# Prompt attention by residue, with inputs split beforehand and outputs scaled from PSUM by VectorE

## Reference

```
q_f, k_f, v_f, logf, dil, gate_a, gate_b = project(x)   # 8 heads of 64; 3 dilated groups (window, r)
# forget-gated prompt attention: c = cumsum(logf)
s = q @ k.T * 64**-0.5 + c[q] - c[k];  o_fox = softmax(s, k <= q) @ v
# dilated prompt attention, groups (128, 1), (512, 4), (2048, 16):
# a query sees keys of its own residue mod r, at most window behind, then groups are merged
o_g, lse_g = band_attn(...);  o_dil = sum_g softmax_g(lse_g) * o_g
h = x + (sigmoid(gate_a) * (o_fox @ Wa) + sigmoid(gate_b) * (o_dil @ Wb)) @ W_out
y = h + relu(rmsnorm(h) @ W_up)**2 @ W_down
```

## Time and profile before

| | us |
|---|---|
| median of 3 runs (range) | 1779.7 (1779.42 to 1780.15) |
| span of the profiled execution | 1779.2 |
| what lies around the span | about 0.5 |
| last sample product to first prompt product | 1068.28 to 1072.42 |
| first product of `finish` | 1255.98 |

### The profile page before, as it was taken

How to read it: one execution, slowest core, us unless ns; L and a number is a source line. 1 busy time by engine, 2 the same in 40 slices (tenths; PEclk the granted TensorE clock), 3 DMA queues, 4 the chain that set the end, 5 groups by cost and what they waited for, 6 DMA issues and landing times. The chain is left out here.

```text
span 1779.2 us, 32332 instructions
## 1 busy us (share of the span) xinstructions
PE 1710.8 (96%) x10749; PEld 1529.3 (86%) x10749; DVE 1086.7 (61%) x2480; ACT 956.5 (54%) x1649; POOL 868.4 (49%) x496
## 2 busy tenths in 40 slices
PE   6999999999889999999999977898999999999998
PEld 5888888899889999899899956888998989899897
DVE  6747556422388888888888877888444514234251
ACT  5444344432368887888888877988314313122230
POOL 1615233300338878778788747775233433333332
PEclk9999999999999999999999998999999999999999
DMA  7386585645889999999999976320645566666662
GB/s 238 106 290 216 202 300 183 207 132 137 253 308 365 344 351 350 353 347 336 355 360 349 316 232 163 91 73 25 215 146 214 235 259 236 259 236 260 236 259 77
DMA packets 191563, 427.76 MB, mean 240 GB/s; under 512 B 22761, under 2 KB 86122, under 8 KB 190002
## 3 DMA queue, kind: packets, MB, share of 16 engines
q1 hardware_dynamic: 187474, 415.29, 66.8%
q10 hardware_dynamic: 2560, 8.39, 1.6%
q0 software_dynamic: 1376, 2.10, 0.5%
HBM read 392.36 MB, written 120.64 MB: 288 GB/s over the span
## 5 line engine op out<-in xcount | busy, mean ns | idle before, releaser
L1086 POOL TENSOR_TENSOR vv_lo<-v_raw,vv_hi 128x1024 fp32r<-128x1024 f32 x178 | 401.4, 2261 | 147.9 <-ACT vv_hi L1175 145.7
L1986 POOL TENSOR_TENSOR w_lo<-w_raw,w_hi 128x2048 fp32r<-128x2048 f32 x39 | 180.1, 4619 | 318.4 <-ACT w_hi L2000 318.4
L1167 ACT ACTIVATE kt_hi<-ktp 128x1024 fp32r<-128x1024 f32 (+1 forms) x192 | 186.2, 970 | 94.0 <-PE ktp L1351 93.2
L1191 DVE TENSOR_TENSOR kt_lo<-ktp,kt_hi 128x1024 fp32r<-128x1024 f32 (+1 forms) x192 | 220.9, 1151 | 8.1 <-ACT kt_hi L1167 6.2
L1365 PE MATMUL s_ps<-kt_hi,q_st 128*128 128x256 f32 (+3 forms) x768 | 205.9, 302 | 0.8 <-DVE mx_parts L1241 0.4
L1351 PE MATMUL ktp<-ident,k_raw 128*128 128x128 f32 x1440 | 192.0, 276 | 8.3 <-DVEq L1182 3.8
L1351 PEld LDWEIGHTS ktp<-ident,k_raw 128*128 128x128 f32 x1440 | 168.6, 142 | 32.7 <-issue 5.6
L707 PE MATMUL acc<-w_hi,xn_hi 128*128 128x512 f32 x480 | 192.4, 401 | 2.4 <-POOL w_lo L340 2.4
L1175 ACT ACTIVATE vv_hi<-v_raw 128x1024 fp32r<-128x1024 f32 (+1 forms) x192 | 191.4, 997 | 6.2 <-PE o_ps L1381 5.7
L1365 PE MATMUL s_ps<-kt_lo,q_st 128*128 128x256 f32 (+3 forms) x768 | 191.0, 282 | 0.0
L707 PE MATMUL acc<-w_lo,xn_hi 128*128 128x512 f32 x480 | 187.7, 391 | 0.0
(11 more groups left out here) (244 smaller groups left out, 4139.4 us busy)
## 6 DMA issues: line engine op xcount, KB each, us to landing
k_raw<-in_cache_fox_k SPq DMA_DIRECT2D x256, 256.0 KB, 4.9
v_raw<-in_cache_fox_v SPq DMA_DIRECT2D x256, 256.0 KB, 4.6
out_win_kv_sample<-in_cache_win_kv SPq DMA_DIRECT2D x32, 2040.0 KB, 9.5
w_raw<-in_w_in SPq DMA_DIRECT2D x32, 1024.0 KB, 5.9
k_raw<-in_cache_win_kv SPq DMA_DIRECT2D x40, 512.0 KB, 9.5
v_raw<-in_cache_win_kv SPq DMA_DIRECT2D x40, 512.0 KB, 8.6
w_raw<-in_w_up SPq DMA_DIRECT2D x16, 1024.0 KB, 5.3
w_raw<-in_w_down SPq DMA_DIRECT2D x16, 1024.0 KB, 5.1
```

Source lines behind the costliest of these rows:

```text
L1086: gp.tensor_tensor(vv_lo[:, slot, 0:tiles, :], v_raw[:, i % RAW_RING, 0:tiles, :], vv_hi[:, slot, 0:tiles, :].bitcast(F32), ALU.subtract). ...
L1167: act.activation(kt_hi[:, slot, :, 0:n], ktp[:, i % 2, :, 0:n], ACT.Copy).then_inc(k_hi, 1)
L1191: ve.tensor_tensor(kt_lo[:, slot, :, 0:n], ktp[:, i % 2, :, 0:n], kt_hi[:, slot, :, 0:n].bitcast(F32), ALU.subtract).then_inc(k_lo, 1)
L1986: gp.tensor_tensor(w_lo[slot][:], w_raw[:, slot, :], w_hi[slot][:].bitcast(F32), ALU.subtract).then_inc(slab_lo_done, 1)
```

## The change

**Residues.** In `project_tokens`, sets 2 and 3 are written with the prompt tokens of one residue mod 4 next to each other (`token_cols`, `turned_cols`). In `attend_prompt` those sets then score only a tile of 128 queries of one residue against the 128 keys of the same residue: 4 tiles a set and head in place of 10. Set 3 (r = 16) keeps a mask inside the tile. A head has 8 + 7 + 10 = 25 tiles, in 7 steps of up to 512 columns (`GROUPS`): two "spread" (sets 2 and 3), two "near" (set 1), three "far" (the forget-gated branch).

**Split inputs.** `project_tokens` stores the transposed queries and keys, and the values, as hi and lo parts. ACT writes y_hi in place of `y_t`; DVE gets a new subtraction of 128x512 out of PSUM a tile for y_lo; for values ACT gets one more copy and DVE one more subtraction a tile. `attend_prompt` splits no input; POOL's queue loads the parts, double-buffered for keys and values. The first pair, with 2 x 1 MB of zeros for the unused halves of the queries, is issued by POOL in `attend_sample` (`first_pair`).

**Outputs.** Probabilities aren't scaled any more. Near and spread have different row orders, so their maxima and sums are merged through DRAM: `send_near`, `take_near`, small operations on DVE, POOL and ACT, `send_shares`, `take_shares`, which brings the reciprocals to all partitions. DVE scales the near and far outputs as it takes them out of PSUM; ACT copies the spread output and POOL scales and adds it, once a pair.

```diff
+SPREAD, NEAR, FAR = 0, 1, 2
+GROUPS = ((SPREAD, (0, 1)), (SPREAD, (2, 3)), (NEAR, (2, 3)), (NEAR, (0, 1)), (FAR, (3,)), (FAR, (2,)), (FAR, (0, 1)))
+S_BANKS, T_BANKS = 3, 2
+SPREAD_BEHIND, NEAR_BEHIND, FAR_BEHIND = (6, 7, 9), (10, 11), (12, 13)
+KEEP_BEHIND, EXP_P_BEHIND, TURN_BEHIND, LOW_BEHIND = 1, 2, 4, 5
 # project_tokens, DVE
+            def turned_rows_lo(s, c, t, by_residue):
+                ve.wait_ge(yt_done, at + 3)
+                ve.tensor_tensor(token_cols(y_lo, t, by_residue), turned_cols(tp[:, slot, :], by_residue),
+                                 token_cols(y_hi, t, by_residue).bitcast(F32), ALU.subtract).then_inc(ylo_done, 1)
...
+                        if c and t < Q_TILES:
+                            turned_rows_lo(s, c - 1, t, by_residue)
+                        if c == 2 and t < Q_TILES:
+                            ve.wait_ge(vhi_done, 4 * s + t + 1)
+                            ve.tensor_tensor(v_lo[:, t, :], acc[:, t, :], v_hi[:, t, :].bitcast(F32), ALU.subtract).then_inc(vlo_done, 1)
 # project_tokens, PE, turn(s, c, t)
+                if at >= 2:
+                    pe.wait_ge(ylo_done, lows_done(at - 2))
 # attend_sample, POOL
+            def first_pair(b, i):
+                if b < DEC_BATCH - 1 or i < LAST:
+                    return
+                done(gp, s_done, group_index(b, LAST))
+                hold(gp)
+                load_keys_of(gp, a, ahead, 0)
+                load_queries(gp, a, ahead, 0, 0)
+                gp.dma_start(ahead["q"][64:128, :, 0].rearrange("p c s n -> p c (s n)"), a["c_zero"].bitcast(F32R)).then_inc(ahead["zeroed"], 16)
+                load_queries(gp, a, ahead, 0, 1)
+                gp.dma_start(ahead["q"][0:64, :, 1].rearrange("p c s n -> p c (s n)"), a["c_zero"].bitcast(F32R)).then_inc(ahead["zeroed"], 16)
 # attend_prompt, SP
+            def send_near(h, i):
+                if i == 0:
+                    sp.wait_ge(exp_done, STEPS * h + 4)
+                    sp.dma_start(a["stat_s"][h].rearrange("c (q p) -> p (c q)", p=P), ...)
...
+            straight(HEADS, STEPS, (6, send_near), (7, take_near), (8, bias_ahead),
+                     (10, send_far), (12, send_shares), (13, take_shares))
 # attend_prompt, POOL
+            def load_values(p):
+                for x, part in ((v_hi, "vh_s"), (v_lo, "vl_s")):
+                    for s in range(SETS):
+                        gp.dma_start(x[:, p % 2, s], src.rearrange(form, t=Q_TILES)).then_inc(v_in[p % 2], 16)
...
+            straight(HEADS, STEPS, (0, mask_diagonals), (0, keys_ahead), (7, queries_ahead), (7, values_ahead), (9, gaps), (10, weights), (11, divide), (15, scale))
 # attend_prompt, ACT
+            straight(HEADS, STEPS, (EXP_P_BEHIND, exponentials), (TURN_BEHIND, turns_hi), (10, gap_exponentials), (10, copy_spread),
+                     (TURN_BEHIND + 1, split_lead))
 # attend_prompt, DVE
+            def copy_near(h, i):
+                if i == 0:
+                    ve.wait_ge(weighed[NEAR], len(NEAR_JOBS) * (h + 1))
+                    ve.wait_ge(share_in, 16 * (h + 1))
+                    ve.tensor_tensor(o_all[rows_of(h), PAIRS + h // 2, 0:SEQ], o_ps[rows_of(h), NEAR, :], share[rows_of(h), 1, :], ALU.mult).then_inc(copied[NEAR], 1)
...
+            straight(HEADS, STEPS, (KEEP_BEHIND, keep), (LOW_BEHIND, turns_lo), (9, invert_far), (9, least_of_both), (11, invert_whole), (14, copy_near), (14, copy_far))
 # attend_prompt, PE
+            straight(HEADS, STEPS, (0, score), (TURN_BEHIND, turn), *(weigh_spread(job) for job in range(len(SPREAD_JOBS))),
+                     *(weigh_near(job) for job in range(len(NEAR_JOBS))), *(weigh_far(job) for job in range(len(FAR_JOBS))))
```

More of the change, by code:

```diff
@@ L1451, in attend_prompt @@
+        v_lo = sb("v_lo3", [P, 2, SETS, Q_TILES, P], F32R)
+        probs = sb("probs3", [P, sum(group_cols(i) for i in range(STEPS))])
+        pt_hi = sb("pt_hi3", [P, P_SLOTS, P], F32R)
+        pt_lo = sb("pt_lo3", [P, P_SLOTS, P], F32R)
+        q, k, masks, bias = (ahead[n] for n in ("q", "k", "masks", "bias"))
+        q_hi, q_lo = q[:, 0], q[:, 1]
+        q_in, k_in, zeroed, masks_in, bias_in = (ahead[n] for n in ("q_in", "k_in", "zeroed", "masks_in", "bias_in"))
         left_hi, left_lo = lead[0], lead[1]
@@ L1713, in split_lead, with exponentials @@
-            def split_lead(p, i):
-                if p < PAIRS - 1 or i < CHUNKS - 1:
+            def exponentials(h, i):
+                kind, units = GROUPS[i]
+                act.wait_ge(kept, STEPS * h + i + 1)
+                if kind == FAR:
+                    after(act, far_inverted, h - 1)
+                for n in units:
+                    x, (least_of, sum_of) = probs[:, prob_cols(i, n)], (stat[:, h % 2, kind, c, n:n + 1] for c in range(2))
+                    last = act.activation(x, x, ACT.Exp, scale=-1.0, bias=least_of, accum_out=sum_of)
+                last.then_inc(exp_done, 1)
@@ L2356, in build @@
         with nc.cleanup_on_exit(), nc.sbuf_tensor("qk_raw3", [P, 2, SETS * SEQ], F32) as qk_raw, nc.sbuf_tensor("o_t", [P, 2, PAIRS, N_SAMPLE], F32) as o_t:
-            pair_in = [nc.alloc_semaphore(f"pair_in3{n}") for n in range(3)]
+            ahead = early_prompt(nc, raw_at)
             early_in = dict(pages=nc.alloc_semaphore("pages_in"), queries=nc.alloc_semaphore("queries_in"),
```

810 lines of the change are left out of this document (411 added, 399 removed).

## The result

The changed kernel takes 1895.2 us (median of four runs, 1888.6 to 1902.4) against 1779.9 for the kernel before, run beside it: a ratio of 1.065, 95% interval 1.061 to 1.069. The forecast was 1761, its range ended at 1786. The profiled execution has a span of 1886.6 us, 107.4 more than before.

What follows compares the result with a forecast made beforehand. PE was taken as the bound, coupled with ACT in the prompt stage. From 1779.2 us, -33 (prompt stage), +13 (end of sample stage) and +2 (projection) gave 1761 us, range 1743 to 1786.

Steps and rivals of the forecast that it cites:

- PE's own work in the prompt stage: Prompt stage: 14.6 us a head, 117 for eight; with 28 of waits, 145 from first score to last sum.
- close race with ACT and DVE: Prompt stage: PE bounds at 14.6 us a head, ACT and DVE 1 to 1.6 below, so waits remain.
- excess: Prompt stage time beyond PE's own work: 36 us before; 28 after, as 8 at start, 15 middle, 5 end.
- The start: Last sample product to first prompt score: 2 us in place of 4.1, since the first score needs no split.
- The end: Last weighted sum to first product of `finish`: 7.5 us in place of 2.0, for two transfers and scaling.
- The round of the weights: Prompt stage, each head: four transfers through DRAM plus small operations, 15 to 22 us, fitting the 22 available.
- Rival 1: Prompt stage: the round, or POOL's issues ahead of it, sets the pace; about 1800 us, slower; chance 0.15.
- The end of the sample stage: POOL's eight early transfers, 6.3 MB, delay `vn` and PE stands: +13 us, bounds +4 and +21.
- bound of an even share: Sample stage's end: both streams share bandwidth evenly, `vn` lands about 1070, +21 us, whole 1769; chance 0.15.
- rival 3: First pair doesn't hold `vn` long and the prompt stage has 8 us fewer waits: 1745 us; chance 0.22.
- The projection: New DVE subtractions and strided PSUM reads in the projection: +2 us, bounds 0 and +7.
- `finish`: Last stage: keeps its instructions and isn't hurried by others, change 0.

Runs made afterwards that it cites:

- e3: Changed kernel without the round through DRAM: near_stat and share loaded once from constants, so prompt outputs are not the reference's; 1785.0 us.
- e4: Changed kernel with POOL's first_pair loads issued three steps later, behind the second load of the new values vn; 1888.3 us.
- e5: e4 with only keys and one head's queries in first_pair, zeros by memset, and first y_lo ahead of w_lo in the projection; 1876.2 us.
- e13: e9 with the changed kernel's DVE order in the projection, and v_hi and v_lo stores behind the next set's weight slab loads; 1794.9 us.
- e9: Changed kernel with fewer pieces, later copies, the smaller first pair behind the new values, and an earlier w_lo in the projection; 1793.3 us.
- e15: e14 with e13's store order, the next pair's values at step 11 instead of 7, and branch slabs loaded after the first head; 1786.0 us.
- e7: Changed kernel without POOL's loads of keys, queries and values for the second to fourth pair; prompt outputs not the reference's; 1867.2 us.
- e12: e2 without POOL's loads for the second to fourth pair; prompt outputs not the reference's; 1810.7 us.
- e2: Changed kernel with fewer, larger pieces in the round's transfers, such as a near store of 512 x 8 bytes instead of 1024 x 4; 1839.1 us.
- e10: e9 with near tiles scored ahead of spread ones in each head, and the store of the shares one step sooner; 1795.4 us.
- e14: e10 with SyncE's store and load of a head's shares ahead of its wait for the next head's near store; 1783.1 us.
- e1: Changed kernel with the load of a head's shares ahead of the next head's near store in SyncE's list; 1880.0 us.

## Why the prediction was wrong, step by step

- **PE's own work in the prompt stage: size right, in part by luck.** First score to last sum was forecast at 145 and is 141.3 without the round (e3). The change without its round is worth 187.7 - 151.4 = 36 us; what fewer tiles, the absent splits and the absent scaling each give was not measured apart. The 145 held 117 of PE's work and 28 of excess, 15 of it waits from a close race with ACT and DVE, at 13.6 and 13.0 us a head. There is no such race: they are busy 88 and 84 us in the 141, 11.0 and 10.5 a head (I had priced the exponentials at the 0.61 of 384 columns; most have 256 and take 0.50). The excess of 24 looks to be something else: 9.0 us of PE's waits for parts of queries and values, and the lower clock, 0.51 and 0.50 in 20 of the first 30 us, where PE gets through 45 and 50 products in 10 us, against 83 at the full level (1165 to 1185 us). The start fits (2 us; 2.2). The end does not: its 7.5 us were for two transfers and the scaling, and e3 has 7.9 with no such transfer, the changed kernel 14.9.
- **The round of the weights: the step that failed.** The sum had no term for it. I priced four transfers at 2.8 to 4.5 us, from loads of 128 and 256 KB, none of them in pieces of 4 bytes, put the small operations at 4, and let "it fits, barely in the worst case" stand. The near store took 11.1 us, the near load 8.2, the store of the shares 4.4 and their load 13.0: about 37 us for four, where I had 11 to 18. From `least` to the shares the small operations alone took 5.9 us at most heads. So the round was 30 to 51 us where 22 were free, and it cost 106.5 us of the stage (e3). I had written beside it that the near store has pieces of 4 bytes and gave that no upper bound. Rows 8 and 9 held no scattered store, so the honest upper end lay open. Rival 1 was the case, with the right sign of it, and its chance of 0.15 was too small; its 1800 was worked out at 6 us a transfer, and they took 9.2 in the mean.
- **The end of the sample stage: sign right, size wrong, 30 in place of 13, outside the bounds of 4 to 21.** The delay by POOL's issues was right (2.8 us; forecast 2 to 5). The bound of an even share counted `vn`'s place in the queue and kept the total rate. The rate fell to some 240 GB/s at 1060 to 1080 us, and e4 shows that the place is worth only 7 of the 30: with `vn` ahead, the window's values are late in its stead. So my rival 3 and my forecast both looked at `vn` alone. The price doesn't go with the bytes in proportion either: behind `vn`, 6.3 MB cost 23 us (e4) and 3.1 MB cost 5 (e5).
- **What I took from the page.** The even share ("DMA: Bandwidth & Descriptors" of the Trainium skill, section Queues, rings and completion order) was nearer than my middle value, yet short by 9 us; that rule says nothing of the total rate. The estimate from its section Anatomy of one DMA, 9 us for four transfers, is a quarter of what the case shows; moreover the Trainium skill gives that fit for transfers issued by POOL, and the round's are SyncE's. The same page of the Trainium skill has a rule that I should have weighed (section Rules for kernel authors): a last dimension that isn't contiguous becomes one descriptor per element. The trace agrees: 1040 packets under 512 bytes during one near store of 1024 elements. It took 11.1 us, 512 pairs 4.9.
- **The projection: size in the bounds (6.7; 0 to 7), cause wrong.** Not DVE's subtractions, but slabs behind stores in SyncE's queue (5.5 of the 6.7, e13). The size is luck, then.
- **`finish`: right,** 523.8 against 523.2 us.
- **The clock: not foreseen.** PE standing at each head brings the granted clock to 0.71 in the stage, 0.95 before. PE is busy 25 us longer with the same products than in e3; how much of the 107 us that is, and how much the wait itself, was not measured apart.

What stays open: why the same transfers of the round take longer in e13 than in e9, how much of the clock is in the round's price, what lowers the rate of the two streams, and whether the moved values or the branch slabs cost e15 its 8 us.

## What to carry to other kernels

When an edit sends small results round through DRAM, price each transfer by its number of pieces and by what stands ahead of it in the same queue, not by its bytes, and if no row shows such a transfer leave the upper end open. Add the waits in the issuing engine's list to the round: a store that is ready still goes behind the wait of the one before it. When a load is moved under another stage whose DMA engines are full, it delays whatever streams beside it, wherever it stands in its own queue: here moving it behind the urgent transfer gave back 7 us, halving its bytes 18 more.

## What the runs showed of the hardware that I had not expected

- 1024 pieces of 4 bytes took 9.7 to 12.2 us as one store with no large load in flight (e7), and 10.4 to 18.9 with them, six of eight under 12 (changed kernel); 512 pieces of 8 bytes, the same 4 KB, 4.2 (e12) and 4.9 (e2) in the median, and 9.0 to 9.7 where another store of pieces and large loads were in flight (e10, e14).
- A load of 384 KB landed, with no large load in flight, in 11.3 us behind 1024 pieces (e7), 6.4 behind 512 (e12), and 4.3 with nothing ahead (last head). Beside large loads it took 13.0 behind 1024 (changed kernel), 6.7 behind 512 (e2) and 6.8 with nothing ahead (e1): there fewer pieces gained as much as a free queue.
- A load of 4 KB took 8.0 to 8.6 us in the median beside large loads of another queue (changed kernel, e2, e9) and 3.4 to 3.7 without them (e7, e12), whether it had 256 pieces or 128. Where it left at another moment of the head (e1, e10) it took 5.1 and 4.3, and single ones 1.5 to 11.4.
- Two large streams together moved 337 to 351 GB/s in the first 10 us, while keys were loading, and then 210 to 265 at a DMA share of 1.2 to 1.3, with queries and zeros for 64 partitions beside the window's values (changed kernel, e4); one alone moved 331 at 0.97. No run tells whether the second stream or the form of its transfers lowers the rate.
